# A hybrid trunk step on one core: three filler pieces of the linear-attention loop are put ahead of the turned keys

## What is computed

```python
def step(s, inp):
    qc, kc, vc, gc = inp
    b = jnp.cumsum(gc, axis=2)
    o_inter = jnp.einsum('bhcd,bhde->bhce', qc * jnp.exp(b), s)
    rel = jnp.where(causal, b[:, :, :, None, :] - b[:, :, None, :, :], -jnp.inf)
    att = jnp.sum(qc[:, :, :, None, :] * kc[:, :, None, :, :] * jnp.exp(rel), axis=-1)
    o_intra = jnp.einsum('bhij,bhje->bhie', att, vc)
    b_last = b[:, :, -1:, :]
    s_new = jnp.exp(b_last[:, :, 0, :])[..., None] * s + jnp.einsum('bhcd,bhce->bhde', kc * jnp.exp(b_last - b), vc)
    return s_new, o_inter + o_intra
...
merged = (gates[..., 0, :] * (o_a @ w_po_a) + gates[..., 1, :] * (o_b @ w_po_b)
          + gates[..., 2, :] * (o_c @ w_po_c))
```

## Time and profile before

| | |
|---|---|
| median of 3 runs | 1991.41 us (1989.2 to 1996.9) |
| the profiled execution's own time | 1994.91 us |
| its span, first to last instruction | 1991.9 us |
| TensorE busy | 1786.1 us, 90% |
| VectorE busy | 987.0 us, 50% |
| ScalarE busy | 741.0 us, 37% |
| GpSimd busy | 198.5 us, 10% |
| mean granted TensorE clock | 0.958 |

### The profile page before, as it was taken

How to read it: one execution, slowest core, us unless ns; L and a number is a source line. 1 busy time by engine, 2 the same in 40 slices (tenths; PEclk the granted TensorE clock), 3 DMA queues, 4 the chain that set the end, 5 groups by cost and what they waited for, 6 DMA issues and landing times. The chain is left out here.

```text
span 1991.9 us, 41977 instructions
## 1 busy us (share of the span) xinstructions
PE 1786.1 (90%) x18403; PEld 1501.9 (75%) x18403; DVE 987.0 (50%) x1779; ACT 741.0 (37%) x1309; POOL 198.5 (10%) x381
## 2 busy tenths in 40 slices
PE   5799888768897999999989989988688889999998
PEld 2799555536664989999989975554566579899998
DVE  1526436597635463334342444466774446433332
ACT  2434435323443343333243443534332343433321
POOL 2000003233300000000000000041422000000000
PEclk9899998979998999999999999998899999999999
DMA  7533222201304445663443432221022244344342
GB/s 247 173 113 119 85 90 92 84 10 45 109 2 149 148 128 157 163 179 98 130 137 109 127 99 88 91 93 48 2 66 88 70 158 121 104 127 127 101 125 81
DMA packets 267949, 213.20 MB, mean 107 GB/s; under 512 B 7226, under 2 KB 259545, under 8 KB 267641
## 3 DMA queue, kind: packets, MB, share of 16 engines
q1 hardware_dynamic: 264816, 203.67, 33.9%
q0 software_dynamic: 2736, 6.80, 1.1%
q10 hardware_dynamic: 216, 0.06, 0.0%
HBM read 207.63 MB, written 2.88 MB: 106 GB/s over the span
## 5 line engine op out<-in xcount | busy, mean ns | idle before, releaser
L583 PE MATMUL bank<-scr_rounded 128*128 128x384 f32 x1344 | 452.4, 337 | 0.0
L583 PEld LDWEIGHTS bank<-scr_rounded 128*128 128x128 f32 x1344 | 253.8, 189 | 1.3
L582 PE MATMUL bank<-scr_rounded 128*128 128x384 f32 (+1 forms) x672 | 227.3, 338 | 13.9 <-ACT scr_rounded L1418 13.3
L582 PE MATMUL bank<-scr_rounded,gate_rounded 128*128 128x384 f32 (+1 forms) x672 | 227.3, 338 | 10.9 <-ACT scr_rounded L1418 9.3
L641 PE MATMUL bank<-h,ring 128*128 128x384 f32 x576 | 212.4, 513 | 14.3 <-DVEq L361 9.9
L587 PE MATMUL bank<-scr_rounded,gate_rounded 128*128 128x384 f32 (+1 forms) x672 | 222.0, 336 | 0.0
L587 PE MATMUL bank<-scr_rounded 128*128 128x384 f32 (+1 forms) x672 | 222.0, 336 | 0.0
L1873 DVE TENSOR_TENSOR scr_rounded<-ring,gate_rounded 128x2048 fp32r<-128x2048 f32 (+3 forms) x65 | 135.4, 2083 | 154.4 <-ACT gate_rounded L1407 153.7
L1873 DVE TENSOR_TENSOR scr_rounded<-ring,scr_rounded 128x2048 fp32r<-128x2048 f32 (+1 forms) x65 | 135.4, 2083 | 137.0 <-ACT scr_rounded L1407 135.3
L641 PEld LDWEIGHTS bank<-h,ring 128*128 128x128 f32 x576 | 108.4, 197 | 93.0 <-issue 35.7
L1407 ACT ACTIVATE gate_rounded<-ring 128x2048 fp32r<-128x2048 f32 (+3 forms) x65 | 113.6, 1747 | 154.3 <-PE bank L587 64.5
(11 more groups left out here) (393 smaller groups left out, 3080.9 us busy)
## 6 DMA issues: line engine op xcount, KB each, us to landing
ring<-in_w_in_dram SPq DMA_DIRECT2D x56, 1024.0 KB, 5.3
ring<-in_w_ada_dram SPq DMA_DIRECT2D x48, 1024.0 KB, 5.3
ring<-in_w_ffn_in_dram SPq DMA_DIRECT2D x88, 512.0 KB, 5.2
ring<-in_w_ffn_out_dram SPq DMA_DIRECT2D x32, 704.0 KB, 4.5
ring<-in_w_out_dram SPq DMA_DIRECT2D x8, 1024.0 KB, 5.0
ring<-in_w_po_a_dram SPq DMA_DIRECT2D x4, 1024.0 KB, 6.0
ring<-in_w_po_b_dram SPq DMA_DIRECT2D x4, 1024.0 KB, 8.1
ring<-in_w_po_c_dram SPq DMA_DIRECT2D x4, 1024.0 KB, 9.3
```

Of the source, the lines that this page charges most:

```text
L582: pe.matmul(o, w_hi[:, k, :], right[0][k], start=k == 0, stop=False)
L583: pe.matmul(o, w_lo[:, k, :], right[0][k], start=False, stop=False)
```

## The change

Three filler steps move. They used to stand ahead of the waits of the loop's pairs 0, 1 and 2; they now stand in the batch ahead of the wait for the scaled keys.

```diff
@@ -818,7 +818,7 @@
                         ins = turn(b[:, 128 * i:128 * i + 128], pb[:, 4 + i, CH * cc:CH * cc + CH])
                     ins.then_inc(psum_ready, 1)
-                fill(6)
+                fill(9)
                 pe.wait_ge(S["gla_scaled"], told("gla_scaled", l, 1))
                 for m, (cc, d) in enumerate(combos):
                     pe.wait_ge(*room())
@@ -840,7 +840,8 @@
                 far = []
                 for n in range(2 * LEVELS):
-                    fill(1)
+                    if n > 2:
+                        fill(1)
                     pe.wait_ge(S["gla_z"], told("gla_z", l, n + 1))
```

## The result

| | before | changed |
|---|---|---|
| median, first timing (4 runs each) | 1992.86 us | 2011.76 us |
| ratio, 95% interval | | 1.0092 (1.0065 to 1.0119) |
| ratio, timed again | | 1.0086 (1.0062 to 1.0110) |
| ratio, a third time | | 1.0056 (1.0035 to 1.0078) |
| span of the first profiled execution | 1991.9 us | 2011.9 us |

The change makes the kernel slower, by 11 to 18 us as the three timings stand, and 15.5 us by their mean. Each ratio is taken against the kernel before, timed beside it. The forecast was 10.9. The first measured time, 2011.8, lies 4 us above the range I gave.

The account below looks back on a forecast made before the run. Bound in this stretch: ScalarE's exponentials, VectorE's four multiplications, then keys, states, pair 0, while TensorE waits. Hold 5.43 + 5.42 = 10.85 us, loop gain 0, clock 0: 1991.4 + 10.9 = 2002.3 us, range 1997.5 to 2007.5.

Parts of the forecast that it names:

- The hold: Ahead of the scaled keys: VectorE's first multiplication waits behind emptying po 4 and po 5, 5.43 and 5.42 us later per layer.
- The loop's gain: Pairs 0 to 2 without their filler steps: gain 0, bound 0.8 us per layer, all of pair 1's lateness.
- The clock: Turned keys and states behind TensorE's idle time: a 1.2 GHz stretch as before, taken as 0, at most 1.2 us more per layer.
- Rival 4: Clock stays up behind the moved steps, giving back 1.6 and 1.7 us: 1998.9 us, chance 0.10.
- worst case for `po` 5: po 5 ahead of the keys at the low clock: at worst 1.8 us more per layer; full clock was taken.
- slower by over 0.5%: Whole kernel: a time from 2001.4 us up, given chance 0.60.
- Rival 1: Unexplained TensorE waits inside the 96-matmul pairs shrink as instruction supply catches up, taking up the shift: 1994.1 us, chance 0.07.
- Rival 2: Pairs 0 to 2 wait for TensorE and VectorE isn't held: -9.4 us, 1982.0 us, faster; chance 0.02.
- Rival 3: Low clock in addition, 1.2 GHz under po 5 and all turned keys and states: 16.9 us, 2008.3 us, chance 0.11.

Follow-up runs that it names:

- e1: Changed kernel, but VectorE empties po 4 and po 5 behind its four key and query multiplications instead of ahead of them; ratio 0.9999 to the kernel before.
- h2: Kernel before with seven thrown-away VectorE additions (the last of half size) ahead of the first multiplication, no filler step moved; ratio 1.0058.
- f4: Changed kernel with five thrown-away matmuls ahead of TensorE's wait for the scaled keys; ratio 1.0056 to the kernel before.
- e2: Changed kernel with VectorE's two emptyings behind the multiplications and ScalarE emptying the ada ahead of its branch C exponentials; ratio 0.9980 to the kernel before.
- g1: Kernel before with five thrown-away matmuls ahead of TensorE's wait for the scaled keys, nothing moved or held; ratio 0.9982.
- g3: Two of the three steps ahead of the keys, pair 2 keeping its step, both engines emptying where they hold nobody; ratio 0.9974 to the kernel before.
- f2: Changed kernel with ScalarE emptying the ada ahead of its four branch C exponentials, VectorE's order left as changed; ratio 1.0075 to the kernel before.
- f3: Changed kernel with nine steps ahead of the keys, but the loop keeps its step ahead of every pair; ratio 1.0095 to the kernel before.
- e4: Kernel before with the three steps taken out of the loop and run at the phase's end, none put ahead of the keys; ratio 1.0043.
- f1: The changed kernel unaltered, timed a second time against the kernel before; ratio 1.0086.
- h3: Second timing of the version with two steps ahead of the keys and nobody held; ratio 0.9976 to the kernel before.
- g2: Kernel before with eight thrown-away VectorE additions ahead of the first multiplication, holding it 7.2 us per layer, no step moved; ratio 1.0078.
- e3: Only one step moved ahead of the keys, from pair 0, with VectorE emptying po 4 there; ratio 1.0028 to the kernel before.
- h1: The changed kernel unaltered, timed a third time against the kernel before; ratio 1.0056.

## Why the prediction was wrong, point by point

**The hold: right.** The hold was forecast at 5.43 and 5.42 us per layer, and measured 5.50 and 5.50 in each of three traces. The order of its parts was right too: bank emptied, 0.15 us to get going (I had 0.05), 2.82 for `po` 5 (2.85), 0.51 to the first multiplication (0.50). Without VectorE's hold (e1) the cost vanishes, with a hold alone (h2) it is there.

**The loop's gain: right.** Taken as 0, with 0.8 as a bound; TensorE is 0.8 us less late at pair 1, and pair 2 comes no sooner behind pair 0 in the first layer and 0.15 us sooner in the second.

**The clock: the first step that failed.** I wrote "so I expect such a stretch again and take 0", with at most 1.2 more per layer. The low level did come again, but over all of turned keys and states: 10.23 us where it was 9.21 and 9.35, +1.0 and +0.9 (in the third trace's first layer -0.1). The term measures +1.9 where I had 0, within its own bound of 1.2 per layer. With it failed the sentence that from the turned keys to pair 2 the distances should be as now. Rival 4 was unlikely for the reason I gave, an idle gap of 4.1 us that stayed (4.12 measured); f4 shows that with the gap filled its price was right: 7.72 us, which is 1.5 and 1.6 below the kernel before where the rival had 1.6 and 1.7. What I overlooked is that the clock term can be had without moving a filler step: the idle time costs 1.5 and 1.6 us already in the kernel before, and that is all that e2, g1 and g3 gain in the stretch.

One reading in the prediction was wrong, though nothing hung on it: the 4.67 us of `po` 0 aren't its time at the low level, since the granted clock over them was 0.61 and not 0.50. The worst case for `po` 5 was thus above 1.8 us.

**The sum and its range.** With 11.0 for the hold and 1.9 for the clock the stretch costs 12.9 us (12.7 and 11.8 in two more traces), 0.65%, which lies in each of the three intervals or on its edge. I forecast 10.9. That alone would have put the forecast at 2004.3 us, within my range. Of the 9.5 us by which the first timing, 2011.8, missed 2002.3, the clock makes 1.9, the hold 0.15, and 1.5 come from the kernel before, whose median was 1992.9 in this timing and 1991.4 in the forecast. The other 6 lie behind the stretch or are scatter. The measured 18 and 17 us stand 4 to 5 above the stretch, more than the 3 us that I allowed for a new set of runs; the 11 us stand 1 below. So the range was too narrow at its upper end. The forecast of slower by over 0.5% stands.

**What lies behind the stretch: the second step that failed, and its cause is open.** The prediction let everything behind the first multiplication slide by 5.4 us and put its growth at nothing; its one rival here had the waits shrink. The mean of the three ratios is 15.5 us, 3 above the stretch's mean of 12.5. In the six traces with VectorE held for over 4 us behind moved steps (the changed kernel three times, f2, f3, f4) pair 0 to pair 13 takes 37.1 to 39.1 us per layer, in the eleven others 34.4 to 38.5; the means are 38.0 and 36.4. With both layers of a trace added up the two groups don't overlap: 74.6 to 77.5 us against 71.2 to 74.3. The timings part in nearly the same way. Ratio less stretch is +5.4, +4.4 and -0.6 us for the changed kernel and +5.3, +7.2 and +3.3 for f2, f3 and f4; all others lie between -2.1 and +0.6, except e4 (+8.7), whose steps went to the phase's end. Each of these differences is uncertain by 4 to 6 us, and f1 to f4 share one timing of the kernel before, the lowest of the five. Neither moved steps without a hold (e1, e2, g3, h3) nor a hold without moved steps (g2, h2) shows the growth; e3, with one step moved and a hold of 1.7 us, doesn't either. I formed the groups only when I had the results, and h1 doesn't fit by its ratio, but scatter alone would hardly sort the traces so. Up to the barrier at the phase's end the growth is still there (126.4 us for both layers on average of the six, 123.3 of the others without e4). Some 3 us of the change thus seem to come from hold and moved steps together; no run tests it.

Part of it are TensorE's waits inside the 96-matmul pairs for nothing that the profile shows, here in the changed kernel's first trace (first layer, then second):

```profile
PE bank L805 <- issue: 5.8, 4, 3.0
...
PE bank L805 <- issue: 5.0, 3, 4.1
```

against 4.5 and 3.6 before and 4.6 and 3.6 in its second trace. Over the six traces they make 5.1 us per layer, over the eleven others 4.2. Rival 1 expected these to shrink; they didn't (the third trace of the changed kernel has 4.2 and 4.3). The traces do show where they stand. Counted from the program's start, all of them above 0.3 us come in all 17 traces behind the same matmul records of TensorE: in the first layer behind the 1952nd, 2080th, 2207th, 2334th and so on, in the second behind the 11224th, 11351st, 11478th and so on, every 127 or 128 records (give or take one or two records). In f4 and g1, where ten records are put in ahead of the pairs of each layer, they keep these counts and so fall ten records earlier in the loop, and twenty in the second layer. So they belong to places in TensorE's instruction stream and not to data that another engine owes; that speaks for the delivery of instructions, which no run here tested. The low clock inside the loop isn't the source: up to pair 8 it costs the changed kernel 0.16 us (see e4). Nor are the missing fillers, since f3 has them. Why the waits are longer where a hold and moved steps meet stays open.

**The other rivals.** Rival 2 (loop bound by TensorE) is refuted by pair 2, and by e1, where VectorE isn't held, the loop lacks the three steps, and the time is as before. Rival 3's clock under `po` 5 did not come: both `po` ran at full pace, 2.85 and 2.82 us.

## What to carry to other kernels

Work that is put into an engine's idle time has consumers. Before moving it, look where the other engines will empty it in their fixed order: here six free matmuls brought two emptyings of 0.55 us in front of a critical multiplication, and the engine stood there for 5.5 us. Mark the hand-over so that what is on the path goes first; two of the three steps, emptied behind it, made the kernel faster (g3, h3). And price idle time of TensorE by the clock behind it, not by its own length: read the granted clock of the stretch that follows.

## What the runs showed of the hardware that I had not expected

- Keeping TensorE fed is worth as much as filler steps well placed: with its wait filled by five thrown-away matmuls, the eight records of turned keys and 32 of states behind it took 1.09 and 1.97 us, against 1.97 and 3.68 at the low level. The stretch from the first multiplication to pair 0 then takes 7.72 or 7.73 us, first and second layer, in all five such traces (e2, f4, g1, g3, h3), and wanders between 9.1 and 10.2 where the clock falls.
- With 9.50 us of idle ahead of them (h2) the same 40 records are no slower than with 4.12 (changed kernel): 9.90 and 10.09 us to pair 0 against 10.23.
- VectorE and GpSimd slowed each other down. VectorE additions of 128x768 took 1.47 to 1.57 us beside GpSimd's differences and 0.96 us alone; two of GpSimd's differences of 128x384 took 1.53 and 1.55 us beside them, and the two earlier ones 0.82 and 0.83 us. Beside ScalarE's exponentials the multiplications of the same size kept their 0.95 us. From g2:

```profile
320.77 0.82 POOL L1298 TENSOR_TENSOR scr<-scr 128x384 f32<-128x384 f32 x1 [19.75 <-DVE scr L2082]
...
321.65 9.54 DVE L2086 TENSOR_TENSOR scr<-scr 128x768 f32<-128x768 f32 x8
...
322.37 1.53 POOL L1298 TENSOR_TENSOR scr<-scr 128x384 f32<-128x384 f32 x1
...
323.86 1.55 POOL L1299 TENSOR_TENSOR scr<-scr 128x384 f32<-128x384 f32 x1
```

- TensorE's waits inside dense runs of small matmuls stand at even distances in its program, every 127 or 128 matmul records, in all 17 traces. Each lasted from nothing to 4.4 us, differently from trace to trace of one kernel.
- Two traces of one kernel, the kernel before, agree to 0.14 us over the stretch looked at here and differ by 4.9 us in the whole span.
